# Three 256-column products per weight tile instead of a 256- and a 512-column one, in the MLP of an f32r kernel

## What is computed

```python
u = rms_norm(h, g_pre_mlp[l])
f = jnp.square(jax.nn.relu(u @ w_up[l])) @ w_down[l]     # w_up 2048 x 8192, w_down 8192 x 2048
h = h + rms_norm(f, g_post_mlp[l])
```

## Time and profile before

| | |
|---|---|
| time, median of 3 runs | 2312.73 us (2312.59 to 2315.18) |
| span of the profiled execution | 2313.0 us |
| TensorE busy | 2152.4 us, 93% |
| VectorE, ScalarE, GpSimd busy | 1626.2, 973.5, 466.8 us |
| mean granted TensorE clock | 0.971 of full |

### The profile page before, as it was taken

The page is one execution under the profiler, slowest core; times in us unless marked ns, Lnnn a source line. Parts: engine busy times, 40 slices in busy tenths (PEclk is TensorE's granted clock), DMA queues, the critical chain, the costliest instruction groups (busy, mean ns, idle before and its releaser), DMA issues.

```text
span 2313.0 us, 35019 instructions
## 1 busy us (share of the span) xinstructions
PE 2152.4 (93%) x12285; PEld 1856.4 (80%) x12285; DVE 1626.2 (70%) x1827; ACT 973.5 (42%) x1205; POOL 466.8 (20%) x364
## 2 busy tenths in 40 slices
PE   6899999999998999799887999979999999999998
PEld 5767788788776888699776878868888888888887
DVE  5796876877785665647999868658666666666654
ACT  5443344566553444343232354345333333333343
POOL 3010010100213111103799303114010010010012
PEclk8899999999999999899998999989999999999999
DMA  7744555455446655454444545544555666556552
GB/s 229 224 124 142 147 164 155 137 158 157 139 142 186 186 185 189 128 174 155 146 136 139 180 134 184 184 153 146 182 182 183 191 188 185 187 187 186 181 182 73
DMA packets 377811, 383.40 MB, mean 166 GB/s; under 512 B 12343, under 2 KB 373733, under 8 KB 377431
## 3 DMA queue, kind: packets, MB, share of 16 engines
q1 hardware_dynamic: 374524, 370.95, 52.4%
q0 software_dynamic: 976, 6.82, 0.9%
q10 hardware_dynamic: 2203, 4.23, 0.5%
HBM read 377.59 MB, written 4.23 MB: 165 GB/s over the span
## 4 chain that ended last, share of the span: by engine, by line
PE 64%; DVE 15%; POOL 9%; issue 7%; ACT 3%; DMA 1%; POOLq 0%; SPq 0%; DVEq 0%; ACTq 0%
PE acc L467 35%; PE acc L466 18%; DVE w_low L407 4%; POOL product L688 4%; PE acc L463 3%; POOL conv L690 2%; ACT w_high L400 2%; PE acc L457 2%; DVE tmp L484 2%; PE acc L459 2%; PE acc L458 2%; PE acc L464 1%; DVE conv L1756 1%; DVE rstd L1504 1%; POOL sumsq L652 1%
## 5 line engine op out<-in xcount | busy, mean ns | idle before, releaser
L407 DVE TENSOR_TENSOR w_low<-stage,w_high 128x1024 fp32r<-128x1024 f32 (+1 forms) x726 | 913.7, 1268 | 568.4 <-ACT w_high L400 550.4
L400 ACT ACTIVATE w_high<-stage 128x1024 fp32r<-128x1024 f32 (+1 forms) x726 | 741.8, 1030 | 969.5 <-PE acc L467 880.6
L467 PE MATMUL acc<-hT,w_high 128*128 128x512 f32 x1395 | 501.4, 398 | 0.0
L466 PE MATMUL acc<-hT,w_low 128*128 128x256 f32 x1395 | 406.4, 291 | 3.3 <-DVE w_low L407 3.3
L467 PE MATMUL acc<-u,w_high 128*128 128x512 f32 x960 | 344.9, 401 | 0.0
L467 PE MATMUL acc<-f_pair,w_high 128*128 128x512 f32 x960 | 341.9, 398 | 0.0
L467 PEld LDWEIGHTS acc<-hT,w_high 128*128 128x128 f32 x1395 | 264.9, 190 | 59.1 <-issue 3.4
L466 PEld LDWEIGHTS acc<-hT,w_low 128*128 128x128 f32 x1395 | 266.6, 191 | 17.9 <-issue 11.5
L466 PE MATMUL acc<-u,w_low 128*128 128x256 f32 x960 | 271.4, 283 | 1.8 <-DVE u L1395 1.8
L466 PE MATMUL acc<-f_pair,w_low 128*128 128x256 f32 x960 | 270.2, 281 | 0.0
L467 PEld LDWEIGHTS acc<-u,w_high 128*128 128x128 f32 x960 | 181.8, 189 | 42.3
(11 more groups left out here) (351 smaller groups left out, 3308.1 us busy)
## 6 DMA issues: line engine op xcount, KB each, us to landing
stage<-in_w_in SPq DMA_DIRECT2D x296, 512.0 KB, 3.7
stage<-in_w_up SPq DMA_DIRECT2D x128, 512.0 KB, 3.8
stage<-in_w_down SPq DMA_DIRECT2D x128, 512.0 KB, 4.4
stage<-in_w_o SPq DMA_DIRECT2D x64, 512.0 KB, 4.6
stage<-in_w_mem_kv SPq DMA_DIRECT2D x16, 512.0 KB, 6.9
stage<-in_w_pool_out SPq DMA_DIRECT2D x16, 512.0 KB, 3.5
stage<-in_w_conv_out SPq DMA_DIRECT2D x16, 512.0 KB, 4.5
stage<-in_w_up_a SPq DMA_DIRECT2D x16, 384.0 KB, 3.3
```

The lines of the kernel that those rows point to most:

```text
L400: act.activation(w_high[:, pr, 0:kt, 0:p.cols], stage[:, slot, 0:kt, 0:p.cols], ACT.Copy).then_inc(high_done, 1)
L407: dve.tensor_tensor(w_low[:, pr, 0:kt, 0:p.cols], stage[:, slot, 0:kt, 0:p.cols], w_high[:, pr, 0:kt, 0:p.cols].bitcast(F32), ALU.subtract ...
L466: pe.matmul(bk[:, 0:T], low, a, start=False, stop=False, skip_group_check=True)
L467: mm = pe.matmul(bk, high, both, start=False, stop=final, skip_group_check=True)
```

## The change

In the MLP alone, a weight tile gets three products of 256 columns into the same PSUM columns. The order of the three differs by quarter: `hl, lh, hh` in the first, `hh, hl, lh` in the second, `hl, hh, lh` in the third, `lh, hh, hl` in the fourth (first letter the weight's part, second the activation's). The 272-column jobs keep their order under the new interface. Since the bank now holds the finished sum in 256 columns, no fold is needed: after a group of `w_up`, ScalarE reads the two banks with a Relu into `tmp` and VectorE squares and splits; after a group of `w_down`, VectorE copies the banks to `y` (first quarter) or adds them to `y` in place, and GpSimd's additions and its zeroing of `y` are gone.

```diff
+HIGH_LAST = ("hl", "lh", "hh")
+HIGH_FIRST = ("hh", "hl", "lh")
+LOW_BETWEEN = ("hl", "hh", "lh")
+HIGH_BETWEEN = ("lh", "hh", "hl")
...
+        def halves_of(pair):
+            return lambda k: (pair[:, k, 0, :], pair[:, k, 1, :])
...
-            order.append((f"w_up{q}", Job(8, [Part(A["w_up_2"], q * D, full, rhs_of(u2), ("pair_ready", 24))], 2)))
-            order.append((f"w_down{q}", Job(8, [Part(A["w_down_2"], 0, full, rhs_of(f_pair), ("f_ready", 8 * q), row0=q * KT)], 2)))
+            terms = (HIGH_LAST, HIGH_FIRST, LOW_BETWEEN, HIGH_BETWEEN)[q]
+            order.append((f"w_up{q}", Job(8, [Part(A["w_up_2"], q * D, full, halves_of(u2), ("pair_ready", 24), terms=terms, width=T)], 2)))
+            order.append((f"w_down{q}", Job(8, [Part(A["w_down_2"], 0, full, halves_of(f_pair), ("f_ready", 8 * q), terms=terms, width=T, row0=q * KT)], 2)))
...
-                        if p.wide:
+                        if p.terms:
                             a, b = p.rhs(k0 + k)
-                            pe.matmul(bk[:, 0:TM], high, b, start=first, stop=False)
-                            pe.matmul(bk[:, 0:TM], low, a, start=False, stop=False)
-                            mm = pe.matmul(bk[:, 0:TM], high, a, start=False, stop=final)
+                            for n_term, term in enumerate(p.terms):
+                                mm = pe.matmul(bk[:, 0:p.width], high if term[0] == "h" else low, a if term[1] == "h" else b,
+                                               start=first and n_term == 0, stop=final and n_term == 2)
                             continue
...
-            def add_down(q):
...
-                    pool.wait_ge(s("down"), q * 8 + g + 1)
-                    d2 = y[:, bass.ds(g * 2, 2), :].rearrange("p a t -> p (a t)")
-                    pool.tensor_tensor(d2, d2, tmp[:, u, 0:2 * T], ALU.add).then_inc(s("down_added"), 1)
...
-            pool.memset(y[:], 0.0).then_inc(s("y_zero"), 1)
...
+            pool.wait_ge(s("h2_sums"), 1)
+            for g in range(8):
+                add_square(40 + g, g % 2, g == 0)
...
-                act.wait_ge(s("down_added"), 2 + 24 + g + 1)
+                act.wait_ge(s("down"), 24 + g + 1)
...
+            def up_relu(q):
...
+                    if q or g >= 2:
+                        act.wait_ge(s("f_ready"), 8 * q + g - 1)
+                    act.wait_ge(acc_free, 2 + group)
+                    act.activation(tmp[:, u, 0:2 * T].rearrange("p (a t) -> p a t", a=2), banks[:, :, 0:T], ACT.Relu).then_inc(acc_free, 1)
...
-                    link(fold(dve, v, banks))
-                    dve.sem_inc(acc_free, 1)
-                    f = tmp[:, u, 0:2 * T]
-                    link(dve.scalar_tensor_tensor(out=f, in0=f, scalar=0.0, in1=f, op0=ALU.max, op1=ALU.mult))
+                    dve.wait_ge(acc_free, 2 + group + 1)
+                    link(dve.tensor_tensor(v, v, v, ALU.mult))
...
-                    dve.wait_ge(s("down_added"), 8 * q + g + 1)
-                    fold(dve, tmp[:, u, 0:2 * T].rearrange("p (a t) -> p a t", a=2), banks).then_inc(s("down"), 1)
+                    d2 = y[:, bass.ds(g * 2, 2), :]
+                    if q == 0:
+                        dve.tensor_copy(d2, banks[:, :, 0:T]).then_inc(s("down"), 1)
+                    else:
+                        dve.tensor_tensor(d2, banks[:, :, 0:T], d2, ALU.add).then_inc(s("down"), 1)
```

More of the change, by code:

```diff
@@ L125, with __init__ @@
 class Part:
-    def __init__(self, w, col0, slabs, rhs, ready=None, wide=False, cols=GROUP, stride=GROUP, row0=0):
-        self.w, self.col0, self.slabs, self.rhs, self.wide, self.cols, self.stride, self.row0 = w, col0, slabs, rhs, wide, cols, stride, row0
-        self.ready = ready
+    def __init__(self, w, col0, slabs, rhs, ready=None, terms=None, width=TM, cols=GROUP, stride=GROUP, row0=0):
+        self.w, self.col0, self.slabs, self.rhs, self.cols, self.stride, self.row0 = w, col0, slabs, rhs, cols, stride, row0
+        self.ready, self.terms, self.width = ready, terms, width
 class Job:
@@ L361, in build @@
             order.append((name, Job(4, [Part(A["w_in_2"], col0, full, lambda k: (uT[:, k, 0, :], uT[:, k, 1, :]), ("pair_ready", 16),
-                                             wide=True, stride=stride)], 2)))
+                                             terms=HIGH_LAST, stride=stride)], 2)))
         order += [
@@ L728, in _ @@
                 add_square(32 + g, g % 2, g == 0)
-            def add_down(q):
-                job = jobs[f"w_down{q}"]
-                def body(i, u):
-                    g = i * job.unroll + u
-                    pool.wait_ge(s("down"), q * 8 + g + 1)
-                    d2 = y[:, bass.ds(g * 2, 2), :].rearrange("p a t -> p (a t)")
-                    pool.tensor_tensor(d2, d2, tmp[:, u, 0:2 * T], ALU.add).then_inc(s("down_added"), 1)
-                    if q == 3 and g >= 1:
-                        add_square(40 + g - 1, (g - 1) % 2, g == 1)
-                if q < 3:
-                    repeat(pool, job.steps, job.unroll, body)
-                    return
-                pool.wait_ge(s("h2_sums"), 1)
-                for g in range(job.steps):
-                    body(g // 2, g % 2)
-                add_square(47, 1)
-            pool.wait_ge(s("h2"), 8)
-            pool.wait_ge(s("h2_part"), 8)
-            pool.memset(y[:], 0.0).then_inc(s("y_zero"), 1)
-            pool.wait_ge(s("y_zero"), 1)
-            pool.sem_inc(s("down_added"), 2)
-            for q in range(4):
-                add_down(q)
+            pool.wait_ge(s("h2_sums"), 1)
+            for g in range(8):
+                add_square(40 + g, g % 2, g == 0)
         @block.scalar
@@ L1044, in residual_rows, with body @@
                     act.activation(rows_h[:, t, r * 512:(r + 1) * 512], aux[:, e % 4, :], ACT.Copy).then_inc(s("h_rows"), 1)
+            def up_relu(q):
+                job = jobs[f"w_up{q}"]
+                def body(i, u, part):
+                    banks, group = group_done(act, job, i, u)
+                    g = i * job.unroll + u
+                    if q or g >= 2:
+                        act.wait_ge(s("f_ready"), 8 * q + g - 1)
+                    act.wait_ge(acc_free, 2 + group)
+                    act.activation(tmp[:, u, 0:2 * T].rearrange("p (a t) -> p a t", a=2), banks[:, :, 0:T], ACT.Relu).then_inc(acc_free, 1)
+                return body
             for q in range(4):
-                rounding(f"w_up{q}", beside=square_residual if q == 0 else None)
+                rounding(f"w_up{q}", up_relu(q), beside=square_residual if q == 0 else None)
                 rounding(f"w_down{q}", last_down if q == 3 else None, residual_rows if q == 3 else None)
@@ L1883, in body @@
                 def body(i, u, part):
-                    banks, _ = group_done(dve, job, i, u)
+                    group, _, _ = job.group(i, u, 0)
                     g = i * job.unroll + u
                     v = tmp[:, u, 0:2 * T].rearrange("p (a t) -> p a t", a=2)
-                    link(fold(dve, v, banks))
-                    dve.sem_inc(acc_free, 1)
-                    f = tmp[:, u, 0:2 * T]
-                    link(dve.scalar_tensor_tensor(out=f, in0=f, scalar=0.0, in1=f, op0=ALU.max, op1=ALU.mult))
+                    dve.wait_ge(acc_free, 2 + group + 1)
+                    link(dve.tensor_tensor(v, v, v, ALU.mult))
                     hi, lo = f_pair[:, bass.ds(g * 2, 2), 0, :], f_pair[:, bass.ds(g * 2, 2), 1, :]
@@ L1907, in _ @@
             for q in range(4):
-                splitting(f"w_up{q}", up_body(q), 3)
+                splitting(f"w_up{q}", up_body(q), 2)
                 splitting(f"w_down{q}", down_body(q))
-                dve.wait_ge(s("down_added"), 2 + 8 * q + 8)
                 if q == 0:
```

## The result

| | median, us | runs | lowest to highest |
|---|---|---|---|
| before | 2312.66 | 4 | 2312.3 to 2315.18 |
| after | 2324.82 | 4 | 2322.11 to 2325.07 |

The ratio is 1.0043, with a 95% interval of 1.0029 to 1.0057: slower by 6.7 to 13.2 us. The time lies above the range of the prediction, and slower had the smallest chance of the three there.

What follows compares the result with a forecast made beforehand. TensorE's pace was taken to bound the MLP, and the engine chain its tail. 2313.0 + 3.9 (tiles) - 2.9 (tail) = 2314.0 us of span, or 2313.7 us as median; range 2303 to 2320 us.

Steps and rivals of the forecast that it cites:

- The pace of a tile: MLP: three 256-column products take 354.8 ns a tile, 352.9 before; over 2048 tiles +3.9 us.
- The loss is per product: MLP rival: what 272-column products lose against 2.4 GHz doesn't shrink with width; 356.6 ns a tile, 2317.4 us; chance 0.14.
- Narrow products keep their own pace: MLP rival: the 512-column product costs extra, so three of 256 take 350 ns; 2303.8 us; chance 0.22.
- A limit by instructions: MLP rival: TensorE's queue can't feed product and load faster than 125.5 ns; tile 376.6 ns, 2358.3 us; chance 0.07.
- A repeated load is left out: MLP rival: the second load of a weight shared by neighbours vanishes, giving 17.8 us; 2296 us; chance 0.04.
- The handover starves TensorE: MLP rival: ScalarE's handover costs 1 us or more per us over 8.5, at up to eight places; chance 0.02.
- The weight load "at nothing": MLP: each new product loads its tile, hidden behind a 256-column product of 0.11 to 0.12 us; costed at nothing.
- What moves between the other engines: MLP: VectorE loses the fold, ScalarE gains a 0.63 us Relu; the handover about 5 us after the group is covered.
- The tail: After the last product: TensorE goes on 2.3 us earlier, small products at full clock save 0.6 us; -2.9 us.
- The sum: Whole kernel: 2313.0 + 3.9 - 2.9 = 2314.0 us of span, 0.3 us above the median, so 2313.7 us.
- What would show it: Profile after: 354.8 ns a tile, equal in all quarters; 14333 products and loads; small products 3.2 us after last big one.

Runs made afterwards that it cites:

- the same-tile job: Changed kernel with other weight loads per MLP job; this job loads the same high weight tile for all three 256-column products: 120.0 ns each, whole kernel 2329.48 us.
- the kernel with the products alone: Kernel before with only the three 256-column products in four orders; VectorE copies instead of folding, GpSimd still adds: 2327.26 us, ratio 1.0048.
- the in-place kernel: Kernel before with its old products; VectorE adds the down-projection to y in place, GpSimd's additions gone: 2312.29 us, ratio 0.9986.
- the first kernel of widths: Changed kernel with products of one width per MLP job, 64 to 264 columns: 2779.17 us (one run).

## Why the prediction was wrong, step by step

**The pace of a tile: the step that failed.** "With a price a for each product and b for each column" two equations gave a = 1.9 ns and b = 0.4546, and 354.8 ns for the new tile. It took 360.0. The form of the model was right from 256 columns up, and its price for a product was mis-sized, 1.9 ns where 13.3 were measured; the two tiles that it was fitted to were not of one kind. The 272-column triple is a stream of one width, and the old tile is a mixture that carries 6 ns of its own. The fit could put that extra only into the column's price, and so took it out of the product's. With streams of one form, 256 against 512 columns, b is (226.7 - 120.0) / 256 = 0.417, the array's 2.4 GHz, and a is 13.3 ns. The prediction had noticed that 0.4546 is above 0.417 and let the fit stand; that was the warning.

The rule of the Trainium skill that it was set beside, "TensorE: Matmul & The Clock Gate", section "Back-to-back issue gap", agrees with the column's price as measured here, and has 2.5 ns where these float32r products have 13.3. The page gives that rule for isolated products; for streams of loads and products it has about 131 ns at 512 columns, where these streams took 226.7.

**The rivals.** "The loss is per product" was the mechanism from 256 columns up, and had 0.14. Its 356.6 ns a tile came from taking 20 ns for 48 columns off the 272-column triple; the step from 272 to 256 columns brought 16 ns (3 x 5.3), so the size was still 3.4 ns too small. "Narrow products keep their own pace" read 0.11 to 0.12 us inside the old tile as the narrow product's pace; in a stream of its own it is 120.0, so the time between two starts in a mixture is not a product's price. "A limit by instructions" had 125.5 ns a product, and the step down to 120.0 at 256 and to 111.7 at 224 refutes that value; a floor does exist, but lower than the products of the change. It could be read from the trace of the kernel before: the one-column products of the earlier trace rows, each with its load, start 112 ns apart at the full clock from the second on. "A repeated load is left out" is refuted by 14333 loads and by the same-tile job. "The handover starves TensorE": TensorE's windows are full, and the kernel with the products alone has the same MLP of 746.0 us.

**The weight load "at nothing".** The reason given, that a load of full width hides behind 0.11 to 0.12 us, is not borne out: 6.7 of the 13.3 ns of a 256-column product go when its weights are 64 columns wide. How much of the price is the load itself was not separated. The 107 ns that the Trainium skill, same page, section "LDWEIGHTS (loading the stationary operand)", gives for 128 columns as an estimate compares with a measured floor of 111.7 ns at full clock and 213.3 at half, and its statement that the number of rows doesn't matter agrees with the 120.0 ns for 64 rows.

**What moves between the other engines.** Right: TensorE waits for nothing, the in-place kernel has the MLP of before, and the products alone have that of after.

**The tail.** Forecast -2.9 us, measured -3.0, in part by luck. The small products began 2.5 us earlier and not 2.3, as VectorE's pass took 0.69 us and not 0.743 and GpSimd's sum 1.26 and not 1.34. They took 1.02 us and not 0.83, though at full clock, as forecast: the earlier trace rows shows seven of the eight, as its window ends before the last one, and all eight take 0.95 us there. So the clock gave back 0.4 us and not 0.6, and the two slips offset each other. Alone, the readout gave 0.9986.

**The sum.** 2313.0 + 3.9 - 2.9 used the profiled span as the time, and the 0.3 us to the medians compares two executions: wherever one execution has both numbers, its time is 1.8 to 3.0 us above its span. So something does lie around the span, other than the section on the time before says; it moved the forecast by little. With the measured terms, +14.0 and -3.0, the medians should differ by 11.0; they differ by 12.2, and the ratio's interval of 6.7 to 13.2 us holds both. The range was too narrow because of its bounds for the tile: 350 ns was read inside a mixture, 356.6 took all of 48 columns at 2.4 GHz off the 272-column tile where only 16 ns came off, and the next one up, 376.6, was left outside as a rival of its own.

**What would show it.** Tile equal in all quarters, 14333 products and as many loads: as said. Tile of 354.8 ns: wrong. Small products 3.2 us after the last big one's end: 3.0 after the transposes' start.

## What to carry to other kernels

Splitting a wide product into narrower ones costs a full fixed price for each one added, also when the columns stay the same; here 13.3 ns in about 120, for a product with its load, and below 256 columns a floor of about 112 ns holds at the full clock. Read such a price only from streams of one form: a fit through two stretches of different make gives prices that reproduce both and need not hold for a third, and here a column's price of 0.4546 ns, above the array's 0.417, was the sign of it. Where widths must be mixed, put those of one width together: 0.24% here for nothing but another order, and with the shorter tail 0.41%.

## What the runs showed of the hardware that was not expected

**A bend at 256 columns.** 192, 224 and 240 columns take 111.7 to 112.0 ns, 256 and 264 take 120.0. Several distances are near a multiple of 6.67 ns, 16 array cycles at 2.4 GHz: 113.3, 120.0, 146.7, 173.3, 206.7, 226.7. As many are not: the floor of 111.7, those of 272 to 304 columns, and those with weights of 32 and 96 columns. A little more width can be free (256 to 264) or cost 8 ns (240 to 256).

**The clock fell when the products got narrow.** In the first kernel of widths, TensorE ran at the full clock in the job of 256 columns and for the first 23 products of the job of 64, which began at 1659.12 us, and then at half:

```profile
1656.00:1660.00 4.00, 4.00 (x37) 4.00 (x36) 1.57 (x2) 2.19 (x3) 0.00 (x0) 1.00 0.62 174
1662.00:1666.00 4.00, 4.00 (x21) 4.00 (x20) 0.67 (x1) 0.00 (x0) 0.00 (x0) 0.50 0.44 135
```

```profile
1659.12 0.28 PE L476 MATMUL acc<-f_pair,w_high 128*128 128x64 f32 x1
1659.23 0.28 PE L476 MATMUL acc<-f_pair,w_low 128*128 128x64 f32 x1
...
1661.57 0.28 PE L476 MATMUL acc<-f_pair,w_high 128*128 128x64 f32 x1
```

From the first to the last of these rows are 22 distances of 111.7 ns.

It stayed at 1.2 GHz through the jobs of 64 and 128 columns, in which the records show TensorE busy throughout, and was back at 1.00 in the job of 192. In those two jobs each product then took 213.3 ns whatever its width, 256 array cycles at 1.2 GHz, and the floor of 111.7 ns at full clock is 268. So the floor goes nearly with the array's clock. Whether the loading of 128 weight columns sets it was not tested: no run has narrower weights at these widths.

**Open.** What the 13.3 ns are made of, as every product here has its own load; why a 512-column product next to 256-column ones takes 230 to 241 ns and not 226.7 (235.8 on average in the kernel before, while its 256-column one takes 117.1); why weights of 32 and 96 columns are dearer than those of 64; the 206.7 ns of 448 columns; and the 1.3 us at the very end of the changed kernel.
